# Multiplying each k/v chunk behind the two adaLN chunks that follow it, in the opening of a two-block kernel

## The reference

```
shift, scale, gate = jnp.split(jax.nn.silu(c) @ ada_w[l] + ada_b[l], 3, axis=-1)
shift_c, scale_c, gate_c = jnp.split(jax.nn.silu(c_ctx) @ ada_w[l] + ada_b[l], 3, axis=-1)
h = rmsnorm(x, norm_g[l]) * (1.0 + scale[:, None]) + shift[:, None]
hc = rmsnorm(xc, norm_g[l]) * (1.0 + scale_c) + shift_c
...
qc, kc, vc, upc, ufc, gc = split_proj(hc @ w_in[l])
q, k, v, up, uf, g = split_proj(h @ w_in[l])
att = latent_attention(q, k, v, kc, vc)
out = merge_branches(att, up, uf, g, pool_w[l], pool_scale[l], fourier_w[l], w_out[l])
x_new = x + gate[:, None] * out
```

## Time and profile before

| | us |
|---|---|
| median of 3 runs | 2319.45 |
| lowest, highest | 2317.92, 2319.51 |
| the profiled execution, its own time | 2317.56 |
| its span in the trace | 2315.7 |
| TensorE (PE) busy in the span | 2237.0 |
| mean granted TensorE clock | 0.992 |

### The profile page before, as it was taken

How to read it: one execution, slowest core, us unless ns; L and a number is a source line. 1 busy time by engine, 2 the same in 40 slices (tenths; PEclk the granted TensorE clock), 3 DMA queues, 4 the chain that set the end, 5 groups by cost and what they waited for, 6 DMA issues and landing times.

```text
span 2315.7 us, 29993 instructions
## 1 busy us (share of the span) xinstructions
PE 2237.0 (97%) x11739; PEld 1831.4 (79%) x11739; DVE 1414.9 (61%) x2216; ACT 1034.6 (45%) x1587; POOL 272.3 (12%) x326
## 2 busy tenths in 40 slices
PE   5989999999999999999999998999999999999998
PEld 2567777778888767678888887888888888888887
DVE  3354543367778365456777777677765777567764
ACT  2232332341422354445554565555544555355553
POOL 1001000000011122100011324111100111001111
PEclk9999999999999999999999999999999999999999
DMA  9885343347665485625575545666566665666653
GB/s 348 309 289 182 122 145 125 121 147 222 232 199 174 151 287 191 206 88 179 185 225 166 179 142 159 191 191 188 184 199 191 188 191 186 198 186 189 192 191 117
DMA packets 322428, 437.14 MB, mean 189 GB/s; under 512 B 13848, under 2 KB 220112, under 8 KB 321264
## 3 DMA queue, kind: packets, MB, share of 16 engines
q1 hardware_dynamic: 316800, 413.19, 55.3%
q0 software_dynamic: 3392, 16.90, 2.0%
q10 hardware_dynamic: 2096, 5.15, 0.6%
HBM read 428.89 MB, written 6.29 MB: 188 GB/s over the span
## 4 chain that ended last, share of the span: by engine, by line
PE 88%; DVE 5%; ACT 3%; issue 2%; DMA 2%; POOL 1%; SPq 0%; ACTq 0%; POOLq 0%; DVEq 0%
PE ps L1398 24%; PE ps L1401 12%; PE ps L1385 9%; PE ps L1387 9%; PE ps L1386 9%; PE ps L1417 5%; PE ps L1419 5%; PE ps L1418 5%; PE ps L1365 2%; DVE SPL L1883 2%; ACT SPL L1631 2%; PE ps L1474 1%; PE ps L1491 1%; DMA RAW<-in_ada_w_dram 1%; PE ps L1481 1%
## 5 line engine op out<-in xcount | busy, mean ns | idle before, releaser
L1883 DVE TENSOR_TENSOR SPL<-RAW,SPL 128x1024 fp32r<-128x1024 f32 x592 | 748.5, 1267 | 534.6 <-ACT SPL L1631 532.2
L1398 PE MATMUL ps<-HS,SPL 128*128 128x512 f32 x2688 | 853.6, 399 | 9.9 <-DVE SPL L1883 8.0
L1631 ACT ACTIVATE SPL<-RAW 128x1024 fp32r<-128x1024 f32 x592 | 622.0, 1055 | 455.6 <-PE ps L1387 175.4
L1401 PEld LDWEIGHTS ps<-HS,SPL 128*128 128x128 f32 x2688 | 506.8, 189 | 119.9
L1401 PE MATMUL ps<-HS,SPL 128*128 128x256 f32 x2688 | 530.0, 279 | 0.0
L1398 PEld LDWEIGHTS ps<-HS,SPL 128*128 128x128 f32 x2688 | 412.3, 189 | 15.5 <-issue 7.1
L1385 PE MATMUL ps<-SPL,HS 128*128 128x512 f32 x960 | 395.9, 412 | 18.0 <-DVE SPL L1883 8.7
L1387 PE MATMUL ps<-SPL,HS 128*128 128x512 f32 x960 | 377.2, 393 | 0.0
L1386 PE MATMUL ps<-SPL,HS 128*128 128x512 f32 x960 | 376.9, 393 | 0.0
L1385 PEld LDWEIGHTS ps<-SPL,HS 128*128 128x128 f32 x960 | 181.8, 189 | 79.7 <-issue 22.7
L1386 PEld LDWEIGHTS ps<-SPL,HS 128*128 128x128 f32 x960 | 181.9, 190 | 41.2 <-issue 6.0
(11 more groups left out here) (295 smaller groups left out, 1835.1 us busy)
## 6 DMA issues: line engine op xcount, KB each, us to landing
RAW<-in_w_in_dram SPq DMA_DIRECT2D x208, 512.0 KB, 4.8
RAW<-in_ada_w_dram SPq DMA_DIRECT2D x192, 512.0 KB, 4.9
RAW<-in_ffn_w_up_dram SPq DMA_DIRECT2D x192, 512.0 KB, 3.6
RAW<-in_w_out_dram SPq DMA_DIRECT2D x96, 512.0 KB, 4.5
RAW<-in_ffn_w_down_dram SPq DMA_DIRECT2D x96, 512.0 KB, 4.2
x_spill<-XT POOLq DMA_DIRECT2D x2, 2048.0 KB, 15.1
XT<-x_spill POOLq DMA_DIRECT2D x1, 4096.0 KB, 15.0
MM<-in_x_dram ACTq DMA_DIRECT2D x2, 1024.0 KB, 11.3
```

Source lines behind the costliest of these rows:

```text
L1398: mm(PS[g.banks[j]][:, :], wr, hh, start=k == 0, stop=False, skip_group_check=True)
L1401: m = mm(PS[g.banks[j]][:, 256:512], wl, hh[:, 0:256], start=False, stop=k == KT - 1, skip_group_check=True)
L1631: act(SPL[:, (n - 1) % NSPL, 0, :], raw_of(i), ACT.Copy).then_inc(s_hi, 1)
L1883: tt(w[:, 1, :], raw_of(s["i"]), w[:, 0, :].bitcast(F32), ALU.subtract).then_inc(s_lo, 1)
```

## The change

A chunk gets a number `behind`: it is multiplied after so many of the chunks that follow it. The k/v chunks kv0 to kv5 get 2. So 25 and 26 are multiplied ahead of kv0 (24), and 30 and 31 ahead of kv1 (29); in the other two stretches likewise 44 and 45, 49 and 50, 63 and 64, 68 and 69. All chunks stay where they were in the load queue. The place of an adaLN chunk counts as free once it is multiplied, not once the position has passed it. The body of `run_chunks` becomes `run_chunk(i)`, otherwise unchanged.

```diff
@@ class Chunk
         self.group, self.kc, self.ap, self.shape, self.then = group, kc, ap, shape, None
+        self.behind = 0
@@ load_ahead
-                    if i >= at["taken" if queue[i].shape else "pos"]:
+                    if i >= at["taken"] if queue[i].shape else i not in after_chunk:
                         return
@@ run_chunks
         def run_chunks(upto):
+
             while at["pos"] < upto:
-                i = at["pos"]
-                run_ahead()
-                c = chunks[i]
...
+                first = at["pos"]
+                n = chunks[first].behind
+                for i in [*range(first + 1, first + 1 + n), first]:
+                    run_chunk(i)
+                at["pos"] = first + 1 + n
+
+        def run_chunk(i):
+            run_ahead()
+            c = chunks[i]
...
@@ start(u)
                 if not u:
                     return cs
+                kv[2 * u - 2].behind = kv[2 * u - 1].behind = 2
                 return cs[:8] + kv[2 * u - 2:2 * u - 1] + cs[8:12] + kv[2 * u - 1:2 * u] + cs[12:] + early[u - 1:u]
```

More of the change, by code:

```diff
@@ L354, in run_chunks @@
-                chunk_multiplied(i)
+                first = at["pos"]
[6 more added lines that the diff above has]
+            c = chunks[i]
+            if c.shape == 1:
+                at["pos"] = i + 1
                 if c.then:
                     c.then()
+                return
+            parts = 2 if c.shape and (c.group.wide or len(c.group.banks) == 4) and c.group.src is None else 1
+            if c.shape == 0:
+                pop_side((2 if i < 8 or i >= 28 else 4) if c.group.side == 2 and c.kc % 2 == 0 else 0)
+            elif c.group.side == 0:
+                pop_pair()
+            else:
+                pop_side(c.group.side)
+            assert str(c.ap) == str(queue[i].ap) and c.shape == queue[i].shape
+            ks = {0: [], 2: range(2 * c.kc, 2 * c.kc + 2), 4: range(4 * c.kc, 4 * c.kc + 4)}[c.shape]
+            inputs = {k: need[c.group.stage](k) for k in ks}
+            half = len(c.group.banks) // parts
+            for part in range(parts):
+                of_part = c.group.banks[part * half:(part + 1) * half]
+                after = use(*of_part) if c.kc == 0 else {}
+                if part:
+                    pop_side(c.group.side)
+                put("mm", i=i, c=c, inputs=inputs, after=after, banks=range(part * half, (part + 1) * half), end=part == parts - 1, src=c.group.src)
+            chunk_multiplied(i)
+            if c.then:
+                c.then()
```

## The result

| | before | after |
|---|---|---|
| median, us (runs of the same chip) | 2317.41 (8) | 2325.03 (8) |
| lowest, highest | 2316.01, 2319.51 | 2321.85, 2327.16 |
| the profiled execution, its own time | 2317.56 | 2326.39 |

The ratio is 1.0031, with a 95% interval of 1.0020 to 1.0041: the change makes the kernel some 0.3% slower. The range of the forecast (2323.2, range 2320.2 to 2326.5) holds 2325.03, but in part by luck, because the median of before stood too high: it was 2319.45 in the three runs shown, and 2317.41, 2317.83, 2317.72 and 2317.68 in sets of 8, 30, 29 and 10. The chance of 0.69 for "within 0.2%" was on the wrong case.

The account below looks back on a forecast made before the run. TensorE, busy 2237.0 of 2315.7 us, was taken as the bound. Late copies at kv2 and kv4 less kv0's gain gave +3.64 us, with +0.6 for clock +4.2; from the median, 2323.2 us was taken, range 2320.2 to 2326.5.

Parts of the forecast that it names:

- within 0.2%: The case that the measured time lies some 0.2% (4.6 us) or less from no change; chance 0.69.
- The new wait: At kv2 and kv4 TensorE waits for ScalarE's late bank copy, +1.91 and +1.90 us; at kv0 it resumes 0.34 us sooner.
- The Trainium skill's rule: Independent matmul groups should rotate through PSUM banks; the change undoes this by removing the k/v chunk between two adaLN groups.
- The ring: In the stretches around the k/v chunks, places are refilled sooner and loads run further ahead; worth nothing.
- the landings: At kv2 and kv4 the chunk and the two adaLN chunks land before TensorE resumes, so they cost nothing.
- the second pair: Two adaLN chunks moved ahead of kv1, kv3 or kv5, inside a stretch without a stop; worth nothing by itself.
- Half clock: Behind the longer stops at kv2 and kv4 TensorE runs at 1.2 instead of 2.4 GHz; +0.6 us, bounds -0.5 to +1.9.
- more half clock: Rival: each longer stop brings a full stretch more at half clock, +1.71 us twice, 2326.5 us; chance 0.20 for one or both.
- The sum: Over the opening: 1.91 + 1.90 - 0.17 = +3.64 us, and +0.6 for the clock, +4.2 us.
- given back: Rival: later TensorE waits of 1.8 and 1.1 us, up to 165 us, shrink by the delay; +0.7 us, 2320.2; chance 0.08.

Follow-up runs that it names:

- a_copy_first: Changed kernel, but the splits of kv0, kv2 and kv4 are listed only when reached, so the bank copy stands ahead of them on ScalarE; 2317.11 us, ratio 0.9992.
- b_again: The kernel before, run and profiled once more without any edit; 2318.46 us, ratio 1.0001 to before.
- second_pairs: Kernel before with only kv1, kv3 and kv5 multiplied behind two adaLN chunks, and the change's refill rule; 2317.36 us, ratio 0.9995 to before.
- a_again: The changed kernel, run and profiled once more without any edit; 2323.27 us, ratio 1.0023 to before.
- first_pairs: Kernel before with only kv0, kv2 and kv4 multiplied behind two adaLN chunks, and the change's refill rule; 2323.62 us, ratio 1.0025 to before.
- turn_inside: Changed kernel, but the transposes step ahead of kv0, kv2 and kv4 is two steps later, at kv2 and kv4 between the chunk's halves; 2324.26 us, ratio 1.0029.

## Why the prediction was right or wrong

**The new wait: right.** TensorE waits for the copy at kv2 and kv4, first shown by the rows at L1461 and then by `a_copy_first`, which removes it. Forecast stops 5.46 and 5.85 us, measured 5.63 and 5.89; ahead of kv0 0.3 us shorter forecast, 0.47 measured. As stops alone, 1.91 + 1.90 - 0.34 = +3.47 was forecast, and 2.08 + 1.94 - 0.47 = +3.55 measured in the first pair of profiles. Over the three profiles with the old order at kv2 and kv4 (before, `b_again`, `second_pairs`) and the four with the new one (after, `a_again`, `first_pairs`, `turn_inside`) the three stops sum to 12.14 and 15.50 us in the mean, +3.36. One detail is less settled than the prediction had it: the chain gives as the copy's releaser an `h2` on VectorE (86.89 to 87.30), which frees a slot of `TMP`; the `h1` ahead of it on ScalarE ends at about the same time. Both stand behind kv2's low part.

**The Trainium skill's rule: right in direction.** The Trainium skill's Perfetto Trace Analysis, section Matmuls, asks that independent groups of matmuls rotate through different PSUM banks. The k/v chunk between two adaLN groups did this, and `turn_inside` shows that, with it gone, the next group itself waits 5.50 us for the bank. `a_copy_first` adds that the copy's place in ScalarE's queue decides the price: 0.83 us with the copy first.

**The ring, the landings, the second pair: right.** TensorE waits for no landing in the changed kernel, and `second_pairs` is -0.5 us. DMA is busier between 58 and 75 us, as forecast (0.92 against 0.77).

**Half clock: the step that failed, by its size.** The term was +0.6 us, on the words "When the clock falls within a stop seems to depend on nothing in the program", with bounds of -0.5 and +1.9. In these runs longer stretches go with longer stops. All nine stops of 5.29 to 5.90 us in the table were followed by 6.83 us at half clock; at kv2 and kv4 in the old order all eight stops (3.52 to 4.34 us) were followed by 3.41. The loss at each of the new stops is 2.86 us in the mean of eight, against 1.71, so +1.15 us each and +2.3 for two, above my upper bound of +0.95 each. With kv0 (-0.3) the opening loses 7.59 in place of 5.55 us in the mean, +2.0. The rival "more half clock" named this and was given 0.20. It is what happened, at both stops, but cheaper than its +1.71 each, since TensorE stands still for the first 0.6 to 1.4 us of each long stretch.

**The sum, again.** Opening, mean of four against mean of three: 102.58 - 96.64 = +5.9 us, of which +3.4 stops and +2.0 clock; 0.5 us I can't assign. Forecast was +4.2. The medians of the four kernels lie 5.4 to 7.6 us above before (mean 6.35). So what lies behind the opening gives nothing back: the rival "given back" (+0.7) is out.

**What the first profile adds.** The two first profiles differ by 8.8 us, 3.3 more than their openings. These stretches are part of it (after, same columns as above):

```profile
489.94:493.35 3.41, 3.41 (x7) 1.99 (x7) 1.82 (x5) 0.76 (x3) 0.00 (x0) 0.54 0.34 130
773.20:780.03 6.83, 5.72 (x28) 5.75 (x29) 4.44 (x5) 1.69 (x2) 0.00 (x0) 0.52 1.02 371
824.40:831.23 6.83, 6.83 (x19) 5.43 (x20) 4.10 (x8) 3.65 (x8) 2.82 (x4) 0.52 0.89 314
971.20:974.61 3.41, 3.41 (x9) 2.14 (x9) 1.54 (x5) 0.72 (x2) 0.00 (x0) 0.54 0.39 132
```

Of these four, the second profile of the same kernel has only a shorter one at 773.70 (3.41 us). Whoever explains the difference of one pair of profiles to the end would explain scatter.

**The chances.** Even with the right mechanism, the case "within 0.2%" stood only as long as the clock term stayed near +0.6: 3.6 + 0.6 is 0.18%, so the forecast lay just under the bound, and any error upward crossed it. 0.59 of 0.67 below it was too much. The step from the profile to the median failed too: that the median lies 1.89 us above the profiled execution, "about one more half-clock stretch", came from three runs, and with sets of 29 and 30 runs it is 0.2 and 0.3 us.

## What to carry to other kernels

When two groups that share a PSUM bank are moved next to each other, look for the copy out of the bank in the queue of the engine that makes it, and count everything ahead of it there; the stop is as long as that, not as the copy. The stops of 3.5 us and more cost more than their length here, and the longest cost most in clock too: price a stop with rows of stops of the same length. If a stop is there because the chunk that is needed was loaded last, try moving its load (here -6.7 to -10.8 us) before moving its multiplication (+5.4 to +7.6).

## What the runs showed of the hardware

- **The longer half-clock stretches went with the longer stops.** Stops of 3.52 to 4.41 us were followed by 3.41 us at half clock in 13 of 14 cases (4.29 us, in `a_again`, was followed by 6.83); those of 4.59, 4.65 and the nine of 5.29 to 5.90 us by 6.83. Between 4.29 and 4.41 us the length of the stop alone doesn't decide.
- **Short stops were seldom followed by any.** In the three kernels with an early load, stops up to 1.73 us left the clock at 1.00 throughout. The pair of some 1.2 and 0.65 us right behind early2, which all kernels have, was followed by 3.41 us at half clock once in the twelve profiles, in `a_copy_first` at 140.90; what decides that stays open.
- **The clock behind the opening scatters.** Between profiles the loss there is 7.3 to 13.7 us, and 7.7 against 13.5 for the same kernel. For the same pair of kernels, medians of 10 and of 8 runs gave +5.4 and +7.6 us.
